# Memory panels: the order of a scan unit's steps against the weight panels' low part (VectorE) and of the gated tile's high part against the unit's exponential (ScalarE)

## The reference, cut to what matters

```python
mem_kv = rmsnorm(mem, mem_norm[i]) @ w_mem_kv[i]            # (256, 1024) @ (1024, 1024), i = 0, 1
# scan, per chunk and group g of 6 heads
seg  = cs[:, :, :, None] - cs[:, :, None, :]
Lmat = jnp.exp(jnp.where(causal, seg, -jnp.inf))
CB   = jnp.einsum("bclgn,bcsgn->bclsg", Cc, Bc)
y_diag = jnp.einsum("bclsgr,bcsgrp->bclgrp", CB[..., None] * Lmat, X)
y_off  = jnp.einsum("bclgn,bcgrpn->bclgrp", Cc, prev) * jnp.exp(cs)[..., None]
y = y_diag + y_off + D * xh                                 # then gated by silu(z), normalised, scaled
```

## Time and profile before

| | us |
|---|---|
| median of 3 runs | 1336.27 (1336.2 to 1336.53) |
| profiled execution | 1336.79 |
| its span | 1335.1 |
| TensorE busy | 1324.6 (99%) |
| VectorE busy | 687.9 (52%) |
| ScalarE busy | 588.6 (44%) |
| GpSimd busy | 114.5 (9%) |
| memory panels (246 to 313 us), VectorE busy | 57.16 of 67.0 |
| memory panels, ScalarE busy | 51.01 of 67.0 |

### The profile page before, as it was taken

One profiled execution on the slowest core, in us unless ns is written; L12 is line 12 of the kernel. 1 busy time (PEld: TensorE's weight loads), 2 busy tenths in 40 slices (PEclk: granted clock), 3 DMA queues, 4 the chain that ended last, 5 costly groups with the idle time before them and its releaser, 6 DMA issues.

```text
span 1335.1 us, 18387 instructions
## 1 busy us (share of the span) xinstructions
PE 1324.6 (99%) x6935; PEld 1093.5 (82%) x6935; DVE 687.9 (52%) x1080; ACT 588.6 (44%) x1105; POOL 114.5 (9%) x131
## 2 busy tenths in 40 slices
PE   9999999999999999999999999999999999999998
PEld 7778888888788888888888898777898888888886
DVE  5586677887436443223443364875474432244333
ACT  6645455676435443213332344765354322133321
POOL 0044352660000000000000000000000000000000
PEclk9999999999999999999999999999999999999999
DMA  7343433243432323233222233112223323322221
GB/s 221 104 126 100 130 103 102 93 163 112 159 109 80 99 93 108 95 127 95 94 98 92 79 100 119 48 64 80 79 81 102 114 98 110 95 94 95 97 100 72
DMA packets 75551, 137.75 MB, mean 103 GB/s; under 512 B 6342, under 2 KB 16854, under 8 KB 75478
## 3 DMA queue, kind: packets, MB, share of 16 engines
q1 hardware_dynamic: 71184, 134.76, 31.2%
q10 hardware_dynamic: 4294, 2.00, 0.8%
HBM read 133.41 MB, written 2.93 MB: 102 GB/s over the span
## 4 chain that ended last, share of the span: by engine, by line
PE 97%; DVE 1%; DMA 1%; ACT 1%; issue 1%; DVEq 0%; ACTq 0%
PE G L1733 64%; PE X L1733 12%; PE X L1756 7%; PE G L1806 3%; PE X L1806 3%; PE X L1912 1%; PE X L1921 1%; PE X L1995 1%; PE X L2210 1%; PE X L2182 1%; PE X L2200 1%; DMA raw<-in_w_mem_kv 1%; PE X L1934 1%; PE X L1974 1%; PE X L1983 0%
## 5 line engine op out<-in xcount | busy, mean ns | idle before, releaser
L1118 DVE TENSOR_TENSOR wlo<-raw,whi 128x1024 fp32r<-128x1024 f32 x207 | 252.6, 1226 | 441.9 <-ACT whi L567 440.8
L567 ACT ACTIVATE whi<-raw 128x1024 fp32r<-128x1024 f32 x207 | 217.7, 1058 | 421.3 <-PE G L1733 209.7
L1733 PE MATMUL G<-uhi,whi 128*128 128x512 f32 x736 | 294.3, 400 | 0.2 <-DVE ulo L1135 0.2
L1733 PE MATMUL G<-uhi,wlo 128*128 128x512 f32 x736 | 287.1, 390 | 0.0
L1733 PE MATMUL G<-ulo,whi 128*128 128x512 f32 x736 | 286.7, 390 | 0.0
L1733 PEld LDWEIGHTS G<-uhi,whi 128*128 128x128 f32 x736 | 138.2, 188 | 31.2 <-issue 1.1
L1733 PEld LDWEIGHTS G<-uhi,wlo 128*128 128x128 f32 x736 | 138.1, 188 | 29.5 <-DVE wlo L1166 0.2
L1733 PEld LDWEIGHTS G<-ulo,whi 128*128 128x128 f32 x736 | 138.3, 188 | 28.4
L1733 PE MATMUL G<-whi,hidhi 128*128 128x512 f32 x256 | 99.6, 389 | 0.0
L1733 PE MATMUL G<-whi,hidlo 128*128 128x512 f32 x256 | 99.6, 389 | 0.0
L1733 PE MATMUL G<-wlo,hidhi 128*128 128x512 f32 x256 | 99.6, 389 | 0.0
(11 more groups left out here) (342 smaller groups left out, 2240.5 us busy)
## 6 DMA issues: line engine op xcount, KB each, us to landing
raw<-in_w_up SPq DMA_DIRECT2D x64, 512.0 KB, 3.8
raw<-in_w_down SPq DMA_DIRECT2D x64, 512.0 KB, 3.5
raw<-in_ssd_w_in SPq DMA_DIRECT2D x20, 512.0 KB, 3.6
raw<-in_w_mem_kv SPq DMA_DIRECT2D x16, 512.0 KB, 3.6
raw<-in_ssd_w_out SPq DMA_DIRECT2D x16, 512.0 KB, 3.5
raw<-in_swa_w_in SPq DMA_DIRECT2D x16, 512.0 KB, 3.8
raw<-in_ssd_w_in SPq DMA_DIRECT2D x16, 384.0 KB, 3.4
csrow<-cs_rows SPq DMA_DIRECT2D x16, 384.0 KB, 4.4
```

What stands on the lines that cost most here:

```text
L567: act.activation(whi[q][:, :, :], raw[q % 2][:, :, :], ACT.Copy).then_inc(hi_done, 1)
L1118: dve.tensor_tensor(wlo[q][:, :, :], raw[q % 2][:, :, :], whi[q][:, :, :].bitcast(F32), ALU.subtract).then_inc(lo_done, 1)
L1733: mm = pe.matmul(o, st, mv, start=(kt == 0 and fresh and not go_on), stop=(q == total - 1 and k == 1), skip_group_check=True)
```

## The change

On VectorE `unit_within` is cut into `unit_segments` and `unit_decayed`. In a memory panel in which a unit starts, `unit_masked` and `unit_segments` now stand ahead of `ahead` (the low part of panel p+3); for the first unit of a group `unit_decayed` does too. For the other units `unit_decayed` stays in panel p+1. On ScalarE, when the next panel turns a gated tile (panels 44 to 52), the unit's exponential is moved from the end of panel p behind the tile's high part in panel p+1; this concerns units 13, 14 and 15. Up to panel 35 the order is as before.

```diff
@@ ScalarE, panel()
-                f = Y0_SLOT.get((p, 0))
-                if f is not None and f < 9:
-                    y0_hi(f)
+                if p in Y0_PANEL:
+                    y0_hi(Y0_PANEL[p])
+                    if p - 1 in UNIT_AT:
+                        unit_exp(UNIT_AT[p - 1])
...
                     if not ahead_of_hi:
                         unit_turned(v)
-                    unit_exp(v)
+                    if p + 1 not in Y0_PANEL:
+                        unit_exp(v)
@@ VectorE
-            def unit_within(v):
+            def unit_segments(v):
...
                 k.then_inc(s_k, 1)
+
+            def unit_decayed(v):
+
                 dve.wait_ge(s_k, v + 1)
                 dve.wait_ge(s_exp, v + 1)
@@ VectorE, panel()
                 v = UNIT_AT.get(p - 1)
-                if v is not None:
-                    unit_within(v)
+                if v is not None and p <= 4 * B_MEM:
+                    unit_segments(v)
+                if v is not None and (p <= 4 * B_MEM or v % NT):
+                    unit_decayed(v)
...
                 v = UNIT_AT.get(p)
-                ahead_of_lo = next_panel is not None and v is not None and v % NT == 0
-                if ahead_of_lo:
+                if v is not None:
                     unit_masked(v)
+                if v is not None and next_panel is not None:
+                    unit_segments(v)
+                    if v % NT == 0:
+                        unit_decayed(v)
                 if next_panel is not None:
                     ahead(*next_panel)
-                if v is not None and not ahead_of_lo:
-                    unit_masked(v)
```

More of the change, by code:

```diff
@@ L83 @@
 Y0_SLOT = {(44 + f, 0): f for f in range(9)} | {(53, 1): 9, (53, 3): 10, (54, 1): 11}
+Y0_PANEL = {44 + f: f for f in range(9)}
 Y0_LO = Y0_SLOT | {(54, 0): 10}
```

## The result

| | before | changed |
|---|---|---|
| median of 20 runs, us | 1336.49 (1336.12 to 1337.95) | 1338.82 (1337.25 to 1339.40) |
| ratio | | 1.0014 (1.0008 to 1.0021) |
| span of the profiled execution | 1335.1 | 1337.1 |
| waits of TensorE in the memory panels | 2.3 | 2.4 |

By the ratio the changed kernel is slower by 1.9 us (1.1 to 2.8), by the medians 2.3, by the spans 2.0. Forecast was +1.2, range -0.5 to +2.6.

The account below looks back on a forecast made before the run. TensorE bounds the kernel, with only 2.3 us of waits to win. Block 11's bank 1 starting 1.8 us late, less 0.6 back at outputs 13, gives +1.2 us: 1336.27 + 1.2 = 1337.5, range 1335.8 to 1338.9.

Parts of the forecast that it names:

- What bounds the kernel: TensorE, busy 1324.6 of 1335.1 us; its two waits at outputs 12 and 13, 2.3 us, are all the change can win.
- Panel 36: Low part 39 behind unit 10's segments ends at 253.5; load 41 starts 3.5 us later, lands at 257.0 to 257.4.
- Panel 38 and 40: Unit 11's start and block 9's key copies, done by 263.8 to 264.1: nothing taken, up to 0.5 if the load lands late.
- L: End of low part 42 on VectorE: 267.0 (before 266.08) with 1.2 us lost beside GpSimd's DI product; bounds 265.9 and 267.4.
- rival 2: A wash: VectorE loses nothing to DI, L 265.9, bank 1 0.65 late, 0.61 back at outputs 13: 1336.3; chance 0.16.
- Panel 41: Decayed 12 ahead of low part 44: outputs 12 start at 274.1, TensorE gains 1.6 us; load 46 starts at 275.4.
- Bank 1 of block 11: Value copy behind high part 46 makes TensorE wait 3.4 us; the bank starts at 280.9, 1.8 us later than before.
- from here TensorE sets the pace: Panels 44 to 52, after bank 1 of block 11 starts 1.8 us late: TensorE paces the rest.
- Rival 3: Slower: chain also binds at panel 40 (0.5), two loads 0.5 late each: +2.7, with panel 48 3.2, 1339.5; chance 0.12.
- Outputs 13: Decayed 13 done at 289.05 against outputs due at 290.4, so TensorE's stall of 0.61 there is gone.
- y0 tiles: Panels 44 to 52: TensorE never waits for one; later low parts y0_lo still end 0.4 to 1 us early.
- The sum: Whole change: +1.8 at bank 1 less 0.6 at outputs 13, +1.2 us, time 1337.5; chance 0.66.

Follow-up runs that it names:

- e9: Changed kernel, but on VectorE only unit 12 moved (masked, segments, low part 44, decayed) and block 10's second value copy ahead of high part 46: 1335.05 against 1336.48, ratio 0.9987.
- e6: Changed kernel, but low part 44 between segments and decayed of unit 12, and units 10 and 11 in their VectorE order of before: 1335.90 against 1336.47 before.
- e2: Changed kernel, but unit 12 in its VectorE order of before (masked, low part 44, segments and decayed in panel 42): 1336.80 against 1336.66 before.
- e5: Changed kernel, but low part 44 stands between segments and decayed of unit 12, not behind both: 1336.53 against 1336.47 before.
- e4: Changed kernel, but ScalarE makes the second half of block 10's value copy ahead of high part 46 (panel 43): 1336.21 against 1336.66 before.
- e8: Kernel before, nothing moved, but five scratch-tile copies on ScalarE ahead of the second half of block 10's value copy: 1338.50 against 1336.47.
- e1: Kernel before with ScalarE's part alone (exponentials of units 13 to 15 behind the next panel's y0_hi): 1336.32 against 1336.66, ratio 0.9998.
- e3: Kernel before, but unit 12 alone has segments and decayed ahead of low part 44; ScalarE as before: 1338.46 against 1336.66, ratio 1.0012.
- e7: Kernel before, nothing moved, but three scratch-tile copies on ScalarE ahead of the second half of block 10's value copy: 1337.44 against 1336.47.
- e10: Changed kernel, but on VectorE only unit 12 moved (masked, segments, low part 44, decayed), value copy not moved: 1335.48, ratio 0.9991.

## Why the prediction was right, and where not

The times in this list are those of the changed kernel's own trace; set on the trace of before at the common mark, each is 0.23 later.

- **What bounds the kernel** (2.3 us of waits are all there is to win): no kernel here won more. The best, e9, won 1.4 (median) to 1.7 (panels).
- **Panel 36**: lo 39 ended at 253.55 (forecast 253.5), load 41 landed at 257.08 (257.0 to 257.4). Right.
- **Panel 38 and 40**: the key copy was done at about 264.7 and TensorE waited (0.42, and 0.84 in all by transposes 12), where I took nothing and at most 0.5. The cause was no late load but exp 11: it waited 1.21 for GpSimd, whose six differences of unit 11 took 7.1 us, and the twelve of units 11 and 12 took 12.84 instead of 10.46. I had carried the place of DI and of the differences over unchanged. "SBUF — State Buffer" of the Trainium skill (Who interferes with whom) lets the second of the two engines wait; that the loss fell on GpSimd fits it, but no run here takes the overlap apart. e6 shows that the order of units 10 and 11 brings it about.
- **L**: 266.0, not 267.0. DI ran at 265.79 and met the gate (L1322, 1.24 instead of 0.56) rather than lo 42. DI took 1.55, and 1.56 before, so what was longer in either overlap is the VectorE instruction; DI itself wasn't stretched. This L is that of rival 2, yet its wash did not come: bank 1 was 1.4 late on the common mark and not 0.65, as L is 266.24 there, lo 44 took 1.64 where I had 1.4, and the clock came on top.
- **Panel 41**: outputs 12 without a wait (right), at 274.58 for 274.1 because of panel 40; load 46 at 274.67 for 275.4. Its step, decayed 12 ahead of lo 44, is what e2 and e5 show to be the cause. The two loads of the chain took 3.89 and 3.62 (3.90 and 3.55 in the working).
- **Bank 1 of block 11**: 280.25 for 280.9, wait 2.01 for 3.4, released by the value copy: the mechanism and its place were right, shown by e4, e5 and e8, and 1.4 us later than before on the common mark where I had 1.8.
- **The step that failed** is "from here TensorE sets the pace". I let it go on at its upper clock. The low clock behind the wait cost 1.58 us that stood in no term and no rival. Rival 3, the only one on the slower side (+2.7 and more), had other reasons.
- **Outputs 13**: 0.69 back, forecast 0.6. ScalarE's part alone gives it (e1), but so does TensorE's lateness without that part (e3, e7, e8), so the forecast's reason isn't proven by it.
- **y0 tiles**: "TensorE never waits for a y0 tile" and the cover of 0.4 to 1 us held in the changed kernel, where TensorE is late. In e2 and e6, with the same low parts behind the segments and TensorE on time, it waits 0.2 us for `y0_lo`.
- **The sum**: +1.4 + 1.58 - 0.69 = +2.3, measured 2.24 in the panels, against +1.8 - 0.6 = +1.2. Bank 1's lateness was overestimated by 0.4 and the clock, 1.58, left out, so the number is nearer than its reasons. That 1338.82 lies just inside the range (its upper end is 1338.9) is luck in part: that end was made up of L at 267.4 and late loads, and neither came. Without the clock the measured terms give +0.7, near 1337.2; the five fastest executions took 1337.25 to 1337.54.

## What to carry to other kernels

A step moved into an engine's idle time can still be dear by what it is put ahead of: follow each instruction that now stands behind it through its buffer, the load, the next engine's queue and whatever else stands in that queue. Put a copy that frees the bound engine's banks ahead of work that waits for a load (2.9 us of the panels in e4), and split a group of moved steps at the one that feeds a load (here segments, low part, product). Price a wait of the matrix engine with the clock behind it, not by its length alone.

## What the runs showed of the hardware

Where TensorE's clock fell to its lower level (0.50, 1.2 GHz), TensorE had waited before, but the fall does not always lie at the same place by the wait. In the changed kernel it came at 280.6, 0.3 us after the wait had ended, in e7 (277.7) and e8 (282.8) some 1.6 us after the end, and in e3 at 279.8, within the wait, 2.45 us after it had begun. In the profiled executions there was no fall in those whose longest wait in the memory panels was 0.91 or less (e2, e4, e5, e6, e9, e10), nor after 1.67 and 1.63 in before and e1. There was one after 1.71 (e7, the low rows lie between 277 and 281), after 1.66 and 1.91 (e8, 283 to 286), after 2.01 (changed, 280.6 to 284) and after 3.19 (e3, 0.50 all through 280 to 286). In the changed kernel the fall cost 1.58 us. The scatter of a kernel's executions goes with it: 0.8 to 1.2 us over 11 runs in each of the six kernels without a wait over 0.91 and in e7, 1.8 to 3.3 us in before, e1, e3 and e8, and 2.15 over 20 runs of the changed kernel. That the upper part of that scatter is executions with a fallen clock fits in size (the medians of the changed kernel's two groups lie 1.5 us apart) but is not shown, as one execution of each kernel is profiled.
